# Two feed-forward layers: gate and up products with the high and low rows of the input side by side in one 512-column matmul

## The reference

```python
D_MODEL = 1024
SEQ = 256
D_FF = 2816

def swiglu(h, w_gu, w_down):
    gu = h @ w_gu
    g, u = jnp.split(gu, 2, axis=-1)
    return (jax.nn.silu(g) * u) @ w_down

f = swiglu(rmsnorm(h, ffn1_pre_g[l]), ffn1_w_gu[l], ffn1_w_down[l])
h = h + 0.5 * rmsnorm(f, ffn1_post_g[l])
...
f = swiglu(rmsnorm(h, ffn2_pre_g[l]), ffn2_w_gu[l], ffn2_w_down[l])
h = h + 0.5 * rmsnorm(f, ffn2_post_g[l])
```

## Time and profile before

| | us |
|---|---|
| three runs | 1665.99, 1671.23, 1664.35 (median 1665.99) |
| the profiled execution | 1665.4 |
| its span, first to last instruction | 1663.9 |
| mean granted clock of TensorE | 0.994 |
| PE busy | 1490.9 (90%) |
| DVE, ACT, POOL busy | 1060.9 (64%), 643.6 (39%), 552.2 (33%) |

### The profile page before, as it was taken

How to read it: one execution, slowest core, us unless ns; L and a number is a source line. 1 busy time by engine, 2 the same in 40 slices (tenths; PEclk the granted TensorE clock), 3 DMA queues, 4 the chain that set the end, 5 groups by cost and what they waited for, 6 DMA issues and landing times.

```text
span 1663.9 us, 20481 instructions
## 1 busy us (share of the span) xinstructions
PE 1490.9 (90%) x8043; PEld 1100.5 (66%) x8043; DVE 1060.9 (64%) x1889; ACT 643.6 (39%) x1016; POOL 552.2 (33%) x607
## 2 busy tenths in 40 slices
PE   7999999999999999999999999998777777777776
PEld 7999898888888899998889886644222222222222
DVE  4655655677675555556655769776666667666655
ACT  5444343787354444444553534322222212222211
POOL 1000000311000000000010046777777776777774
PEclk9999999999999999999999999999999999999999
DMA  8555545334344355566444469999999999999997
GB/s 293 178 178 193 187 152 177 102 102 152 115 154 149 129 187 192 178 189 199 132 127 138 154 239 365 385 412 412 411 412 411 411 412 381 412 411 412 411 411 319
DMA packets 199945, 431.95 MB, mean 260 GB/s; under 512 B 20773, under 2 KB 114090, under 8 KB 199850
## 3 DMA queue, kind: packets, MB, share of 16 engines
q0 software_dynamic: 73728, 268.47, 40.5%
q1 hardware_dynamic: 123456, 159.92, 29.6%
q10 hardware_dynamic: 2666, 2.26, 0.5%
HBM read 429.55 MB, written 1.05 MB: 259 GB/s over the span
## 4 chain that ended last, share of the span: by engine, by line
PE 52%; POOL 17%; DVE 10%; DMA 9%; issue 7%; ACT 5%; ACTq 0%; DVEq 0%; POOLq 0%
PE ps L407 52%; POOL GS L2612 10%; POOL RAW L2612 5%; DVE WL L1716 3%; DMA GS<-in_peer_v_dram,AR 2%; ACT WH L1214 2%; DMA AR<-in_peer_v_dram,AR 2%; POOL AR L2612 2%; DMA RAW<-in_peer_v_dram,AR 2%; DMA RAW<-in_peer_u_dram,AR 1%; DMA GS<-in_peer_u_dram,AR 1%; DVE H L1758 1%; DVE XN L1753 1%; DVE XL L1772 1%; DVE AR L1980 0%
## 5 line engine op out<-in xcount | busy, mean ns | idle before, releaser
L1716 DVE TENSOR_TENSOR WL<-RAW,WH 128x2048 fp32r<-128x2048 f32 x143 | 327.9, 2293 | 232.1 <-ACT WH L1214 231.5
L407 PE MATMUL ps<-XH,WH 128*128 128x256 f32 (+1 forms) x1448 | 418.8, 289 | 12.3 <-DVE XL L1772 5.1
L407 PE MATMUL ps<-XL,WH 128*128 128x256 f32 (+1 forms) x1448 | 411.0, 284 | 0.0
L407 PE MATMUL ps<-XH,WL 128*128 128x256 f32 (+1 forms) x1448 | 410.9, 284 | 0.0
L407 PE MATMUL ps<-GS,AR 128*128 128x512 f32 x576 | 281.3, 612 | 81.4 <-DMA GS<-in_peer_v_dram,AR 70.3
L1214 ACT ACTIVATE WH<-RAW 128x2048 fp32r<-128x2048 f32 x137 | 262.4, 1915 | 181.7 <-PE ps L407 179.9
L407 PEld LDWEIGHTS ps<-XH,WH 128*128 128x128 f32 x1448 | 279.4, 193 | 21.0 <-issue 9.5
L407 PEld LDWEIGHTS ps<-XL,WH 128*128 128x128 f32 x1448 | 279.5, 193 | 3.2 <-issue 2.4
L407 PEld LDWEIGHTS ps<-XH,WL 128*128 128x128 f32 x1448 | 279.5, 193 | 0.0
L407 PEld LDWEIGHTS ps<-GS,AR 128*128 128x128 f32 x576 | 99.2, 190 | 259.5 <-issue 223.7
L2451 DVE CUSTOM_DVE_ANT_0 GS<-GS,ps 128x1024 f32<-128x1024 f32 x146 | 177.8, 1218 | 124.6 <-DMA GS<-in_peer_u_dram,AR 124.2
(11 more groups left out here) (372 smaller groups left out, 1988.9 us busy)
## 6 DMA issues: line engine op xcount, KB each, us to landing
RAW<-in_ffn_w_gu_dram SPq DMA_DIRECT2D x44, 1024.0 KB, 5.1
RAW<-in_w_in_dram SPq DMA_DIRECT2D x39, 1024.0 KB, 5.2
RAW<-in_ffn_w_down_dram SPq DMA_DIRECT2D x22, 1024.0 KB, 4.9
RAW<-in_w_out_dram SPq DMA_DIRECT2D x12, 1024.0 KB, 4.9
RAW<-in_xa_wkv_dram SPq DMA_DIRECT2D x8, 1024.0 KB, 5.3
RAW<-in_w_peer_q_dram SPq DMA_DIRECT2D x8, 1024.0 KB, 7.6
RAW<-in_xa_wq_dram SPq DMA_DIRECT2D x4, 1024.0 KB, 6.3
RAW<-in_xa_wo_dram SPq DMA_DIRECT2D x4, 1024.0 KB, 4.9
```

The costliest lines, as they stand in the source:

```text
L407: return nc.tensor.matmul(out_, lhsT, rhs, start=start, stop=stop, skip_group_check=True)
L1716: nc.vector.tensor_tensor(conv(1, k, kt), v, conv(0, k, kt).bitcast(F32), ALU.subtract).then_inc(S["lo"], 1)
```

## The change

The high and the low input become one tensor XX with two planes, and `mm2` takes both planes of a block as 512 moving columns with the high weights: high x high lands in columns 0 to 255 of a bank, low (of the input) x high (of the weights) in 256 to 511. The third product, 256 columns with the low weights, is added to the first half. Since gate and up now need a whole bank each, they have fixed banks: gate r in 4 + r, up r in 6 + r, no longer taken from `b47`. The two halves of a bank are added afterwards: ACT copies the second half to SBUF (`gate_part`, `up_part`), DVE adds the first, and only then come the scaling, and the product with silu. A bank is free again when its add is done (`halves`). The row scales and the gains go through banks 0 and 1.

```diff
-        YY, XH, XL = [early.enter_context(nc.sbuf_tensor(n, [P, k, T], F32R)) for n, k in (("YY", 32), ("XH", 8), ("XL", 8))]
+        YY = early.enter_context(nc.sbuf_tensor("YY", [P, 32, T], F32R))
+        XX = early.enter_context(nc.sbuf_tensor("XX", [P, 2, 8, T], F32R))
...
+    XH, XL = XX[:, 0, :, :], XX[:, 1, :, :]
...
+        def mm2(b, w, c, start, stop):
+
+            mm(two(bank[b]), w[0], XX[:, :, c, :], start, False)
+            return mm(bank[b][:, 0:256], w[1], XH[:, c, :], False, stop)
...
-                bb = [b47(), b47()]
                 for q in range(2):
                     w = piece(8, ("gate_mm", NFF * f + i + 1) if q == 0 else ("gu", 22 * f + 2 * i + 2))
                     for r in range(2):
-                        at_bank["gu", 22 * f + 2 * i + r] = bb[r]
-                        pe.wait_ge(*freed[bb[r]])
+                        b = 4 + 2 * q + r
+                        pe.wait_ge(*freed[b])
...
-                            ins = mm3(bank[bb[r]][:, q * 256:q * 256 + 256], wcols(w, c, r * 128, 128),
-                                      (XH[:, c, :], XL[:, c, :]), c == 0, c == 7)
+                            ins = mm2(b, wcols(w, c, r * 128, 128), c, c == 0, c == 7)
+                        freed[b] = (S["halves"], both(f, i, r, q))
...
                         if i == 0 and q == 1 and r == 0:
-                            row_scale(name, 6)
+                            row_scale(name, 0)
                             if f == 0:
-                                gains()
+                                gains(1)
...
+                gate_part(f, i, 0)
+                gate_part(f, i, 1)
                 hi()
                 silu(f, i, 0)
+                silu(f, i, 1)
+                up_part(f, i, 0)
+                gated_hi(f, i, 0)
                 if 0 < i < NFF - 1:
                     hi()
-                gated_hi(f, i, 0)
+                up_part(f, i, 1)
                 if i == NFF - 1:
                     hi()
-                silu(f, i, 1)
                 gated_hi(f, i, 1)
...
+            nc.scalar.activation(sg[j % 4], bank[4 + r][:, 256:512], ACT.Copy).then_inc(act.own, act.mark("gate_part"))
...
+            nc.scalar.activation(sgu[j % 4], bank[6 + r][:, 256:512], ACT.Copy).then_inc(act.own, act.mark("up_part"))
...
                 gate_scaled(f, i, 0)
-                gated(f, i, 0)
-                if i == NFF - 1:
-                    gated_lo(f, i, 0)
                 gate_scaled(f, i, 1)
                 if i:
                     lo()
-                if i < NFF - 1:
-                    gated_lo(f, i, 0)
+                gated(f, i, 0)
+                gated_lo(f, i, 0)
+                if 0 < i < NFF - 1:
+                    lo()
                 gated(f, i, 1)
+                if i == NFF - 1:
+                    lo()
                 gated_lo(f, i, 1)
...
+            nc.vector.tensor_tensor(sg[j % 4], bank[4 + r][:, 0:256], sg[j % 4], ALU.add).then_inc(S["halves"], 1)
+            dve.wait_ge(S["halves"], both(f, i, r, 0))
+            nc.vector.tensor_tensor(sg[j % 4], sg[j % 4], RB["ffn1"], ALU.mult).then_inc(S["gscaled"], 1)
...
+            nc.vector.tensor_tensor(sgu[j % 4], bank[6 + r][:, 0:256], sgu[j % 4], ALU.add).then_inc(S["halves"], 1)
+            dve.wait_ge(S["halves"], both(f, i, r, 1))
             dve.wait_ge(act.own, act.nth("silu", J + 1))
...
+            nc.vector.tensor_tensor(sgu[j % 4], sgu[j % 4], sg[j % 4], ALU.mult).then_inc(S["gated"], 1)
```

More of the change, by code:

```diff
@@ L387, in body, with both @@
     GATES = {max(5, 16 * m - 18): m for m in range(1, 16)}
+    def both(f, i, r, up):
+        return 4 * (NFF * f + i) + 2 * up + r + 1
     def pe_program():
@@ L617, in pe_program @@
         pe.wait_ge(S["gain0"], 16)
-        nc.tensor.transpose(bank[7][:, 0:8], AR[0:8, 0:128], ident[0:8, 0:8]).then_inc(pe.own, pe.mark("gain_t"))
+        nc.tensor.transpose(bank[7][:, 0:8], AR[0:8, 2048:2176], ident[0:8, 0:8]).then_inc(pe.own, pe.mark("gain_t"))
         freed[7] = (S["pg"], 1)
@@ L1960, in dve_program @@
         dve.wait_ge(S["rb_sqrt"], 1)
-        nc.vector.reciprocal(sqb, sqb).then_inc(S["rbc"], 1)
-        dve.wait_ge(S["rbc"], 1)
+        nc.vector.reciprocal(sqb, sqb).then_inc(dve.own, dve.mark())
+        dve.wait_ge(dve.own, dve.n)
         def attention_low(j):
@@ L2345, in choose_first @@
             dve.wait_ge(act.own, act.nth("gate_e", 1))
-            nc.vector.reciprocal(x["r"], x["s"]).then_inc(S["gate_r"], 1)
+            nc.vector.reciprocal(x["r"], x["s"]).then_inc(dve.own, dve.mark("gate_r"))
             yield
```

56 lines of the change are left out of this document (30 added, 26 removed).

## The result

The changed kernel takes 1673.08 us, median of 15 runs (1670.90 to 1679.62), against 1664.89 for the kernel before on the same chip (15 runs, 1661.45 to 1671.23). The medians lie 8.2 us apart; the ratio over all these runs is 1.0053, 95% interval 1.0041 to 1.0064. The profiled execution took 1671.18 us (span 1669.8), 5.8 more than that of before. The forecast was 1668.5, 3.1 above the profile of before, in a range of 1659 to 1675.

What follows compares the result with a forecast made beforehand. PE was taken to bound the kernel, by the number of matmuls times their spacing. -8.5 + 5.3 + 0.4 - 0.7 + 2.1 + 4.5 = +3.1 us on the profiled 1665.4 gave 1668.5 us, range 1659 to 1675.

Steps and rivals of the forecast that it cites:

- The matmuls: Each block's three 256-column matmuls (360.0 ns) become a pair of 347.9 ns; 704 blocks, 8.5 us less.
- Rivals C and D: C: the pair takes 333 ns, total 1660 us, chance 0.12. D: it takes 360 ns, total 1676 us, chance 0.13.
- Pass 0: First pass of both layers: piece 3's splitting comes late, PE stands 3.1 us instead of 0.4; together +5.3 us.
- the timetable: Pass 0 times from G, the first gate piece's end: `hi` of piece 3 from G + 10.6, `lo` to G + 14.8.
- Pass 3: In ffn1, exp starts 0.5 us later ahead of a splitting for which PE already waits 1.33 us; +0.4 us.
- the last down piece: Its wait for the last low half (0.33 us, 0.4 with the restart) goes; -0.7 us over both layers.
- the start of ffn2: The first gate product takes bank 4 and waits until DVE has copied all of XL; +2.1 us.
- The clock: Three breaks over 2.27 us, in pass 1 of each layer and at ffn2's start, halve the clock; +4.5 us, bounds 0 and 4.5.
- Rival B: The clock holds through the breaks; the sum is -1.4, total 1664 us, chance 0.17.
- Steady passes: Delays of 0.4 to 0.5 us stay under the margin and cost nothing; passes 16.6 us apart instead of 16.98, without waits.

Runs made afterwards that it cites:

- e7_grouped: The change with a bank's eight 512-column products first, then its eight of 256, instead of alternating; 1670.46 us, ratio 1.0035 to the kernel before.
- e1_contig: The change with XX laid out block by block, so a block's 512 moving columns are one run; 1765.65 us, ratio 1.0033 to the kernel before.
- e4_three: The change with its halves and split additions, but products as three 256-column matmuls; 1679.93 us, ratio 1.0081 to the kernel before.
- e3_pass0: The change with piece 3 split in pass 0, ahead of the up work, instead of in pass 1; 1761.03 us, ratio 1.0003 to the kernel before.
- e2_turn_bank: The change with the ffn2 turn going through banks 4, 5, 6, 7 in order; 1764.86 us, ratio 1.0029 to the kernel before.
- e8_fill_short: The change with idle matmuls of constants before the waits, 3 in pass 1 of each layer, 4 at ffn2's start; 1674.80 us, ratio 1.0050 to the kernel before.
- the 20 runs above: Unedited kernel before, run beside two later groups of follow-up kernels: 14 runs at mean clock 0.994 or more, median 1663.95 us; 6 at 0.990 to 0.992, 1669.8 us.
- the grouped kernels: e7_grouped (ratio 1.0035 to the kernel before), and the change with the edits of e2_turn_bank, e3_pass0 and e7_grouped together (1665.68 us, ratio 0.9990).

## Why the prediction was nearly right, point by point

**The matmuls.** Mis-sized: a pair takes 353.0 ns, not 347.9, and a pair saves 7.0 ns, not 12.1. 704 pairs by 7.0 ns give 4.9 us instead of 8.5, the largest miss of a term, 3.6 us. I had added the spacings of two rows that each hold one shape; `e7_grouped` gives 3.6 of the 5.1 ns back by removing the alternation, `e1_contig` nothing by joining the data. Rivals C and D are both out: the pair is neither 333 nor 360 ns. The 2.5 ns a matmul that the Trainium skill gives (TensorE: Matmul & The Clock Gate, part 1) are not what the earlier trace rows show, and the dropped matmul was worth 7 ns: here the measurement decides.

**Pass 0.** Right in mechanism and size: 2.67 and 2.83 us of waiting against 0.25 before in either layer, +5.0 for +5.3. `hi` of piece 3 came at G + 10.2 where the timetable had G + 10.6, the low half ended at G + 14.5 for G + 14.8. `e4_three` shows that the wait belongs to the copies and split additions and not to the width (2.42 and 2.6 us without it; the rest is the pieces that get shorter), `e3_pass0` that the order in the lists makes about half of it: 1.3 us stay, in front of the down piece.

**Pass 3, the last down piece, the start of ffn2.** Pass 3 waits 1.52 us for 1.33, +0.2 (forecast +0.4). The wait before the last down piece is gone in both layers, -0.7 as forecast. From the last transposes to the first product of `ffn2` it is 4.72 us instead of 2.37, +2.35 for +2.1; `e2_turn_bank` takes it all away, so bank 4 was the cause.

**The clock.** The sum came near by luck, the places did not. I had three drops of 1.5 us, one behind each break over 2.27 us, after one row of the kernel before. The break in pass 1 of `ffn1` had none behind it, in any of the three profiles of the change; the two of `ffn2` cost 4.1 us (`e8_fill_short`), not 3.0, because the second lasts longer. One drop less and a longer one made up for each other. The rule itself doesn't hold: the very break of the earlier trace rows stands in the changed kernel, as long as before, and its clock stays at 1.00 behind it (window 406 to 412 us), while it drops at 210 us behind a break of 1.12 us that the kernel before has as well, without a drop. Timeline of PE:

```profile
405.34 1.10 PE L413 MATMUL ps<-AR 128*128 128x64 f32 x8 [2.27 <-DVE AR L2030]
```

So the length of a break alone does not tell whether half clock follows; what does is open. In all, the 6.9 us of the last landmark less 2.0 (-4.9 + 5.0 + 0.2 - 0.7 + 2.35) leave 4.9, for a forecast of 4.5. 4.1 of these are measured as the clock's. Of the other 0.8, 0.3 lies between the first two landmarks, where each kernel has one drop, and the rest belongs to no experiment. Rival B, that the clock holds, is out by the windows of 578 to 608 us; `e8_fill_short` shows what it would have given.

**Steady passes.** Right that no splitting is late in them: they are 16.79 us apart without waits. 16.6 was forecast, by the same mis-sized pair.

**What the sum left out.** By one profile each, forecast +3.1, measured +5.8: 3.1 + 3.6 for the pair, less 1.0 behind `ffn2`, and 0.1 of small terms of both signs. By medians it is +8.2. The 2.4 between are in no landmark: the profiled run of the kernel before lies 0.5 us above its median, that of the change 1.9 below. Which stages make the other runs of the change longer was not profiled. Six of its 15 runs belong to its lower group by mean clock (1676.8 us), against 12 of 43 of the kernel before in the two groups that ran at full speed, too few to call it a difference. Against the medians of the 20 runs above (1663.95 and 1669.8), the two groups of the change are 8.3 and 7.0 us slower, near the 6.9 of the last landmark. So the runs do not show that the change acts on the stages behind `ffn2`, whose code is the same.

## What to carry to other kernels

A product that is saved on a full engine is worth what two neighbouring starts become apart, not the columns of one shape plus those of another; time the new sequence in its new order. Ask what has to be done behind the cheaper product, and look for the place where the lists of the side engines are already tight (here the first pass and the first piece after a change of stage), since the rest has margin. And count a break of TensorE with what can follow it: here waits of 3.4 and 2.8 us cost 4.1 us more at half clock, and idle matmuls inside the same breaks took just that away. But one earlier drop does not make a rule for the next: look at several profiles of one kernel, and measure a stage from a mark inside it, since the first gate piece, the same code in all but the grouped kernels and `e4_three`, takes 6.8 to 9.0 us from profile to profile of the changed kernel and its variants.
